# First projections on unscaled tokens: row factors applied in the evictions, bias rows copied out before the first projection's evictions

## The chip, the cores and the metric

The kernel runs on one core of a Trainium2 chip. The metric is the device time in microseconds (us) of one execution of the whole program. TensorE (PE) multiplies matrices into eight PSUM banks of 128 x 512 words. ScalarE (ACT), VectorE (DVE) and GpSimd (POOL) work beside it, and SyncE (SP) issues most transfers. Every engine goes through its own instructions in order, and engines wait for each other by semaphores.

## The reference, cut to what matters

Two transformer blocks over 512 tokens of width 1024, in 32-bit floats. The change touches the start of the first block:

```
h = rms_norm(x, norm_mix)            # x * rsqrt(mean(x*x) + eps) * gain
proj = h @ w_in
qa, ka, va, qg, kg, vg, glr, rg = split(proj)
o_a = moba_attention(qa, ka, va, rp_table)
log_a = log_sigmoid(glr @ w_gate_up + b_gate) / 16
o_g = gla_chunked(qg, kg, vg, log_a)
o_g = rms_norm(o_g, g_norm) * silu(rg)
x = x + concat(o_a, o_g) @ w_out
```

The mean is over the 1024 columns of a token, so the factor of the norm is one number for each token. A product with the weights is linear in the tokens, so that number can be multiplied in before the product or after it. Behind this come the gated linear attention, the two attentions, a cross attention and a wide MLP, and then the second block; none of that is changed.

## The kernel before

**Products.** Every 32-bit product is made of three fast ones. An operand is split into a high part (ACT copies it into `act_hi` or `w_hi`) and a low part (DVE subtracts: `act_lo`, `w_lo`), and the helper `product` issues high by high, high by low and low by high, one line each (L1211, L1212, L1213). A projection over 1024 rows takes 8 chunks k of 3 matmuls for each of 4 banks.

**Weights.** A group of 512 weight columns comes in four units, two chunks k each. The first group (units 0 to 3) is loaded at the start into `w_first`. Later units go through the two slots of `w_raw`: SP loads unit n into a slot when the count `lo_w` says that the low part of unit n - 2 is made (L1167 to L1172). ACT makes the high part (L1607), DVE the low part (L1918). So a late low part makes a late load two units on.

**Order.** `make_schedule` writes one list of steps, and `walk` has each engine go through the same list and do its part of every step. A step on which an engine has nothing to do costs it nothing, and one on which it waits holds up all that it has behind. The steps at the start are:

1. `scale` for each of four token tiles: ACT squares and sums the tile (L1720), takes logarithm and exponential (L1621, L1622), and DVE writes the scaled tile into `y` (L2024).
2. `start` 0: high and low part of weight unit 0.
3. `turn` with `of="opening"`: PE transposes the four scaled tiles (L1353), behind each tile's wait, with filler matmuls ahead of each (`warm`, L1219: 20, 5, 5, 5). ACT takes each of the 8 banks into `act_hi` (L1780), DVE into `act_lo` (L2079).
4. `start` 1: weight units 1 to 3 and the small gate weights.
5. `gemm` glaqk (the q and k of the linear attention), four banks together: chunk k is done for all four banks, then chunk k + 1. PE waits for `act_lo` of the chunk and, every second chunk, for the next unit's `lo_w`. In its first step ACT and DVE split units 4 to 7, those of the next group, vg. Each bank's eviction is behind that, on ACT for banks 0 and 2 (L1632) and on DVE for banks 1 and 3 (L1948).
6. `relbias`: PE multiplies the table of relative biases into bank 7 (L1374). DVE copies the rows out (L2103) and fills the rest (L2105). POOL first issues three loads (L2399, L2400, L2349), then writes the rows to DRAM, spreads them there into `skew_dram` (1536 KB, L2408) and later loads the skewed rows.
7. `glr`: 24 matmuls into bank 4; DVE copies them (L2084).
8. `vg`, first step: PE waits until glaqk has left bank 0 (`begin`), and for units 4 to 7 as its chunks come to them. Then the gate (PE L1369), the levels of the linear attention, and rg, qa, ka and va.

Of the kernel before, what the change touches and what calls it, by code (L numbers as in the profile page):

```python
# [27 lines left out]
F32 = mybir.dt.float32  # L28
# [3 lines left out]
ALU = mybir.AluOpType  # L32
AX = mybir.AxisListType

P = 128
# [94 lines left out]
class Step:  # L130


    def __init__(self, kind, banks, fill, *, n=0, h=0, p=None, out=None, major=None, src=None, dst=None, rows=KC,
                 half=0, first=False, splits=(), ready=None, bank=0, blk=0, mid=None,
                 after=None, tiles=TT, gains=(), chunks=(), row=None, row_n=0, qk_ready=None,
                 of=None, fused=(), units=(), tiles_free=(), held=None, roped=None, packed=None, rstd=None, xn=None, hi=None, xrows=None, smax=None, merged=None, nmax=None, part=None, sum_a=None, sq=None, nth=0, halved=False, mode=None, made=None, splits_lo=None, yg=None, banks_of=(0, TT), mean=None, sq_sum=None):
# [17 lines left out]
        self.nmax = nmax  # L154
# [3 lines left out]
class Schedule:  # L158
# [139 lines left out]
    def bank_steps(self, out, major, src, rows=KC, banks=4, halves=1, ready=None, blk=0, mid=None, dst=None, p=None,  # L298
             after=None, fused=False, pairs=False, by_tile=False, halved=None, of=None, in_parts=False, banks_at=None):
# [10 lines left out]
        for i in range(steps):  # L310
# [23 lines left out]
            else:  # L334
# [7 lines left out]
                          ready=ready if i == (1 if pairs else steps - 1 if fused else 0) else None, bank=bank, nth=b, halved=halves_ready, blk=blk, mid=mid, dst=dst, p=p,  # L342
# [100 lines left out]
def make_schedule():  # L443
# [24 lines left out]
    def transposed(tiles, gains, dst, src, of=None):  # L468

        chunks = [4, 5, 6, 7, 0, 1, 2, 3] if src == "mix" else list(range(KC))  # L470
        st = s.add("turn", range(KC), {"hi": KC}, tiles=tiles, gains=gains, dst=dst, src=src, chunks=chunks,
                   ready=all_out() if src == "mix" else None, of=of)
        return [(chunks.index(c), st.fill[chunks.index(c)], 1) for c in range(KC)]
# [362 lines left out]
def two_blocks(nc, a, out):  # L836

    s = make_schedule()
    with ExitStack() as ctx:
# [58 lines left out]
        decay = const("decay", [2, TT])  # L898

# [104 lines left out]
        bias_dram = nc.dram_tensor("bias_dram", [A_HEADS, REL], F32).ap()  # L1004
        skew_dram = nc.dram_tensor("skew_dram", [A_HEADS, P, REL], F32).ap()
# [33 lines left out]
        bias_made = sem("bias_made")  # L1039
        x_back = [sem(f"x_back{tt}") for tt in range(TT)]  # L1040
# [69 lines left out]

        def each(ap, n):

            return ap.unsqueeze(2).broadcast_to([ap.shape[0], ap.shape[1], n])
# [17 lines left out]
        def copies_of(st):  # L1131

            b, half = st.nth, st.half
            full = psum[:, st.bank, :]
            if st.out == "kx":
                return kx[:, 4 * st.blk + b, :], psum[:, st.bank, 0:M], 1.0, b % 2 == 0
            if st.out == "glaqk":
                return qk_g[:, b, :], full, G_DK ** -0.5 if b < 2 else 1.0, b % 2 == 0
            if st.out == "vg":
                return vg[:, b, :], full, 1.0, b % 2 == 0  # L1140
            if st.out == "va":
                return va[:, b, :], full, 1.0, b % 2 == 0
            if st.out == "qa":
                return qa[:, b, :], full, A_DIM ** -0.5, b % 2 == 0
            if st.out == "ka":
                return ka[:, b, :], full, 1.0, b % 2 == 0
# [61 lines left out]
        def _(pe):  # L1208
# [16 lines left out]
            def gemm(st, turn):  # L1225
# [10 lines left out]
                for k in range(st.rows):  # L1236
                    tile = k // 2 + st.half * (st.rows // 2)
                    if (st.first or st.fused) and k % 2 == 0:

                        pe.wait_ge(lo_w, at(st.units[tile][0], turn, 1))  # L1240
# [11 lines left out]
                    if k % 2 == 1 and tile in st.tiles_free:  # L1252
                        mm.then_inc(tile_done, 1)

# [57 lines left out]
            def handle(st, turn):  # L1312
# [27 lines left out]
                elif k == "turn":  # L1340
                    in_turn = lambda tt: (0, 1, 2, 4, 5, 6, 7, 3) if tt == 0 else range(KC)
                    for n, tt in [(n, tt) for tt in range(st.tiles) for n in in_turn(tt)]:
                        if st.of == "opening" and n == 0:
                            warm((20, 5, 5, 5)[tt])
# [3 lines left out]
                        if n == 0 and st.of in (None, "opening"):  # L1348
# [3 lines left out]
                        rows = y if st.of in (None, "opening") else x  # L1352
# [234 lines left out]
        def _(act):  # L1587
# [36 lines left out]
            def gemm(st, turn):  # L1624
# [5 lines left out]
                if plain is not None and plain[3]:  # L1630
                    filled()
                    act.activation(plain[0], plain[1], ACT.Copy, scale=plain[2]).then_inc(bank_free[b], 1)  # L1632
# [3 lines left out]
                elif st.out == "rg":  # L1636
                    filled()
                    act.activation(sg[:, b, :], psum[:, b, :], ACT.Sigmoid).then_inc(sig_made, 1)
# [40 lines left out]
            def handle(st, turn):  # L1679
# [31 lines left out]
                elif k == "scale_rms":  # L1711
# [9 lines left out]
                    rms(slice(tt, tt + 1), D, rstd_made)  # L1721
                elif k == "rms_x":
# [182 lines left out]
        def _(dve):  # L1905
# [32 lines left out]
            def gemm(st, turn):  # L1938
# [7 lines left out]
                if plain is not None and not plain[3]:  # L1946
                    filled()
                    dve.tensor_scalar(plain[0], plain[1], plain[2], None, ALU.mult).then_inc(bank_free[b], 1)  # L1948
# [4 lines left out]
                elif st.out == "rg":  # L1953
                    dve.wait_ge(sig_made, b + 1)
                    dve.tensor_tensor(sg[:, b, :], psum[:, b, :], sg[:, b, :], ALU.mult).then_inc(bank_free[b], 1)
# [31 lines left out]
            def handle(st, turn):  # L1987
# [93 lines left out]
                elif k == "glr":  # L2081
                    dve.wait_ge(bank_done[4], at(st.fill[0], turn, 1))
                    dve.wait_ge(bias_out, 16)
                    dve.tensor_copy(glr_t[:], psum[0:G_RANK, 4, :]).then_inc(bank_free[4], 1)  # L2084
# [16 lines left out]
                elif k == "relbias":  # L2101
                    dve.wait_ge(bank_done[7], at(st.fill[0], turn, 1))
# [237 lines left out]
        def _(pool):  # L2340
# [14 lines left out]
            def handle(st, turn):  # L2355
                k = st.kind
                if k == "tsum":
# [227 lines left out]
```

## Time and profile before

| | |
|---|---|
| median of 3 runs | 1590.48 us (1589.95 to 1591.76) |
| profiled execution, its own time | 1588.72 us |
| its span, first to last instruction | 1586.9 us |
| PE busy | 1561.5 us, 98% |
| DVE, ACT, POOL busy | 994.7, 662.9, 488.1 us |
| mean granted TensorE clock | 0.998 |

PE is busy for nearly the whole span, so what matters in a stretch is when PE can go on. Of the 25.4 us in which it isn't busy, the first 3.18 us lie ahead of its first instruction. Matmuls overlap in the trace: a 128 x 512 one is listed with 0.39 us, and the next starts 0.23 us after it.

### The profile page before, as it was taken

The numbers are of one execution on the slowest core, as the hardware profiler recorded it, in microseconds if no ns is written. First come the engines' busy times: TensorE is split into PE (matmuls) and PEld (weight loads), VectorE is DVE, ScalarE is ACT, GpSimd is POOL, SyncE is SP. The second block draws the span as 40 slices with busy tenths as digits, with TensorE's granted clock in tenths as the row PEclk, the third lists the DMA queues.
The fourth block names the chain that finished last, engine by engine and source line by source line (L and its number), as shares of the span: only waits on it lengthen the run. The fifth ranks groups of instructions, "written<-read, shape, count | busy, mean of one in ns | idle before, by whom it ended". The sixth has DMA issues, their size and how long they took to land.

```text
span 1586.9 us, 21097 instructions
## 1 busy us (share of the span) xinstructions
PE 1561.5 (98%) x7783; PEld 1308.9 (82%) x7783; DVE 994.7 (63%) x1191; ACT 662.9 (42%) x1087; POOL 488.1 (31%) x284
## 2 busy tenths in 40 slices
PE   8999989999999999999999999999999999999998
PEld 7788888888788888888888898878887988888886
DVE  5453876345477777776664747366355677777765
ACT  5352555244354443443533333634324454434432
POOL 1442000000037777762310000020014047777732
PEclk9999999999999999999999999999999999999999
DMA  6422135221312233214232122243334322213133
GB/s 242 136 80 80 41 106 179 88 80 53 133 53 107 106 107 106 106 55 153 92 106 81 54 93 83 78 162 106 98 135 137 135 107 97 88 53 123 75 109 120
DMA packets 44997, 164.34 MB, mean 104 GB/s; under 512 B 5584, under 2 KB 5800, under 8 KB 44272
## 3 DMA queue, kind: packets, MB, share of 16 engines
q1 hardware_dynamic: 40608, 144.82, 27.9%
q0 software_dynamic: 4304, 18.36, 3.3%
q8 instruction: 56, 0.92, 0.2%
q14 instruction: 29, 0.24, 0.0%
HBM read 158.88 MB, written 5.85 MB: 104 GB/s over the span
## 4 chain that ended last, share of the span: by engine, by line
PE 86%; DVE 6%; ACT 3%; issue 2%; DMA 2%; POOL 0%; DVEq 0%; SPq 0%; ACTq 0%
PE banks L1211 27%; PE banks L1213 26%; PE banks L1212 26%; DVE w_lo L1918 2%; DMA w_raw<-in_weights 2%; ACT w_hi L1607 1%; PE banks L1508 1%; PE banks L1387 1%; PE banks L1328 0%; PE banks L1570 0%; PE banks L1353 0%; PE banks L1546 0%; DVE nmax L2197 0%; PE banks L1497 0%; PE banks L1460 0%
## 5 line engine op out<-in xcount | busy, mean ns | idle before, releaser
L1211 PE MATMUL banks<-act_hi,w_hi 128*128 128x512 f32 (+1 forms) x1088 | 413.4, 380 | 2.9 <-DVE act_lo L2079 2.9
L1918 DVE TENSOR_TENSOR w_lo<-w_raw,w_hi 128x1024 fp32r<-128x1024 f32 x216 | 286.0, 1330 | 204.8 <-ACT w_hi L1607 202.5
L1213 PE MATMUL banks<-act_hi,w_lo 128*128 128x512 f32 (+1 forms) x1088 | 410.0, 377 | 0.0
L1212 PE MATMUL banks<-act_lo,w_hi 128*128 128x512 f32 (+1 forms) x1088 | 409.8, 377 | 0.0
L1607 ACT ACTIVATE w_hi<-w_raw 128x1024 fp32r<-128x1024 f32 x216 | 227.2, 1059 | 260.9 <-DMA w_raw<-in_weights 200.4
L1211 PEld LDWEIGHTS banks<-act_hi,w_hi 128*128 128x128 f32 x1088 | 204.8, 188 | 40.7 <-issue 2.3
L1213 PEld LDWEIGHTS banks<-act_hi,w_lo 128*128 128x128 f32 x1088 | 204.8, 188 | 37.9
L1212 PEld LDWEIGHTS banks<-act_lo,w_hi 128*128 128x128 f32 x1088 | 204.9, 188 | 36.5
L1211 PE MATMUL banks<-w_hi,a_hi 128*128 128x512 f32 x400 | 157.7, 394 | 2.3 <-DVE sums_y L2013 0.9
L1212 PE MATMUL banks<-w_lo,a_hi 128*128 128x512 f32 x400 | 155.9, 390 | 0.0
L1213 PE MATMUL banks<-w_hi,a_lo 128*128 128x512 f32 x400 | 155.8, 390 | 0.0
L1211 PE MATMUL banks<-w_hi,act_hi 128*128 128x512 f32 x352 | 139.8, 397 | 0.6 <-POOL act_lo L2391 0.6
L1213 PE MATMUL banks<-w_hi,act_lo 128*128 128x512 f32 x352 | 137.7, 391 | 0.0
L1212 PE MATMUL banks<-w_lo,act_hi 128*128 128x512 f32 x352 | 137.6, 391 | 0.0
L1918 DVE TENSOR_TENSOR w_lo<-t,w_hi 128x1024 fp32r<-128x1024 f32 x36 | 87.3, 2450 | 37.7 <-ACT w_hi L1607 37.7
L1211 PEld LDWEIGHTS banks<-w_hi,a_hi 128*128 128x128 f32 x400 | 75.1, 188 | 24.6 <-DVE sums_y L2013 4.0
L2365 POOL TENSOR_TENSOR t<-w_down 128x1024 f32<-128x1024 f32 x12 | 39.3, 3278 | 171.9 <-DVE act_lo L2079 171.8
L1918 DVE TENSOR_TENSOR w_lo<-w_down,w_hi 128x1024 fp32r<-128x1024 f32 x48 | 81.2, 1725 | 14.8 <-ACT w_hi L1607 14.8
L1213 PEld LDWEIGHTS banks<-w_hi,a_lo 128*128 128x128 f32 x400 | 75.1, 188 | 15.9
L1212 PEld LDWEIGHTS banks<-w_lo,a_hi 128*128 128x128 f32 x400 | 75.1, 188 | 15.0
L1211 PEld LDWEIGHTS banks<-w_hi,act_hi 128*128 128x128 f32 x352 | 73.9, 210 | 13.8 <-issue 2.0
L1213 PEld LDWEIGHTS banks<-w_hi,act_lo 128*128 128x128 f32 x352 | 73.9, 210 | 11.4
(370 smaller groups left out, 2418.4 us busy)
## 6 DMA issues: line engine op xcount, KB each, us to landing
w_raw<-in_weights SPq DMA_DIRECT2D x216, 512.0 KB, 3.6
w_down<-in_weights SPq DMA_DIRECT2D x48, 512.0 KB, 6.5
wide<-share_dram POOLq DMA_DIRECT2D x3, 1024.0 KB, 7.0
x_tok<-in_x SPq DMA_DIRECT2D x4, 512.0 KB, 5.2
w_first<-in_weights SPq DMA_DIRECT2D x4, 512.0 KB, 8.9
x_tok<-in_x POOLq DMA_DIRECT2D x4, 512.0 KB, 4.8
x_dram<-x_tok POOLq DMA_DIRECT2D x1, 2048.0 KB, 8.1
x_tok<-x_dram POOLq DMA_DIRECT2D x1, 2048.0 KB, 8.7
```

Source lines behind the costliest of these rows:

```text
L1211: pe.matmul(out_ap, lhs[0], rhs[0], start=start, stop=False)
L1212: pe.matmul(out_ap, lhs[0], rhs[1], start=False, stop=False)
L1213: return pe.matmul(out_ap, lhs[1], rhs[0], start=False, stop=stop)
L1387: mm = pe.matmul(psum[:, b, n * P // 2:(n + 1) * P // 2], lev[st.n % 2][rows, pair, tt * P:tt * P + P], right[rows, pair, tt, :, 1, :], st ...
L1508: mm = pe.matmul(psum[:, b, tt % 2 * M:tt % 2 * M + M], qx[:, 2 * st.h + e, tt * P:tt * P + P], kx[:, 2 * st.h + e, :], start=(e == 0), st ...
L1607: act.activation(w_hi[:, slot, :], landed(kind, raw), ACT.Copy).then_inc(hi_w, 1)
L1918: dve.tensor_tensor(w_lo[:, slot, :], landed(kind, raw), w_hi[:, slot, :], ALU.subtract).then_inc(lo_w, 1)
L2365: pool.tensor_tensor(t1[:], w_down[:, 1, :], w_down[:, 0, :], ALU.subtract).then_inc(sum_w, 1)
```

## The change

The steps `scale` of the tokens go. PE transposes `x` itself as soon as a tile has landed, with 10, 3, 3 and 3 fillers. A new step `rms_first`, behind `start` 1, has ACT make the row factors `rstd_x`, and POOL write them to DRAM and load them back as a row on every partition (`rstd_row`). Evictions then multiply them in: the token-major ones (vg, va, rg) by a column of `rstd_x`, the others (glaqk, qa, ka, glr) on DVE by `rstd_row`, so that banks 0 and 2 of these move from ACT to DVE. DVE's part of `relbias` becomes a step of its own, `bias_out`, in the list ahead of the glaqk steps, while the step that PE and POOL act on stays behind them. In glaqk's first chunk PE does the products of the high parts for all four banks first, once `act_hi` and `w_hi` are there, and then the two others (`first_rows`).

```diff
-    for tt in range(TT):
-        scale("x", tt, "x")
     s.add("start", n=0, splits=[s.split_of(u, []) for u in s.coming[0:1]])
-    act_ready = norm("norm_mix", "act", of="opening")
+    act_ready = transposed(TT, ["norm_mix"] * KC, "act", None, "opening")
     s.add("start", n=1, splits=[s.split_of(u, []) for u in s.coming[1:4]])
-    s.gemm("glaqk", "T", "act", ready=act_ready, fused=True)
-    s.add("relbias", (7,))
+    s.add("rms_first")
+    bias = s.add("relbias", (7,))
+    s.items.pop()
+    s.add("bias_out", of=bias)
+    s.gemm("glaqk", "T", "act", ready=act_ready, fused=True, turned=s.turned_hi)
+    s.items.append(bias)
     qk_ready = ready()
...
+            def first_rows(st, turn):
+                unit, slot = st.units[0]
+                pe.wait_ge(hi_made, at(st.turned, turn, 1))
+                pe.wait_ge(hi_w, at(unit, turn, 1))
+                for n, (x_, w) in enumerate(((act_hi, w_hi), (act_lo, w_hi), (act_hi, w_lo))):
+                    if n == 1:
+                        wait_ready(pe, st.ready[0:1], turn)
+                    if n == 2:
+                        pe.wait_ge(lo_w, at(unit, turn, 1))
+                    for one in st.fused:
...
-                            warm((20, 5, 5, 5)[tt])
+                            warm((10, 3, 3, 3)[tt])
...
+                        elif n == 0 and st.of == "opening":
+                            pe.wait_ge(x_in[tt], 16)
...
+                elif k == "rms_first":
+                    for tt in range(TT):
+                        act.wait_ge(x_in[tt], 16)
+                        then(act.activation(y[:, tt, :], x[:, tt, :], ACT.Square, accum_out=sumsq[:, tt:tt + 1]))
+                    then(act.activation(lnv[:, 0:TT], sumsq[:, 0:TT], ACT.Ln, bias=eps[:, 0:1], scale=1.0 / D))
+                    act.activation(rstd_x[:], lnv[:, 0:TT], ACT.Exp, scale=-0.5).then_inc(first_rstd, 1)
...
+                    if st.out in ("glaqk", "qa", "ka"):
+                        dve.wait_ge(spread_in, 16)
+                        dve.scalar_tensor_tensor(by_tile(plain[0]), by_tile(plain[1]), plain[2], rstd_row[:].rearrange("q (p t) -> q t p", t=TT),
+                                                 ALU.mult, ALU.mult).then_inc(bank_free[b], 1)
...
-                elif k == "relbias":
-                    dve.wait_ge(bank_done[7], at(st.fill[0], turn, 1))
+                elif k == "bias_out":
+                    dve.wait_ge(bank_done[7], at(st.of.fill[0], turn, 1))
                     dve.tensor_copy(bias_row[0:A_HEADS, 0:NEAR], psum[0:A_HEADS, 7, 0:NEAR]).then_inc(bank_free[7], 1)
...
+                if k == "rms_first":
+                    pool.wait_ge(first_rstd, 1)
+                    pool.dma_start(rstd_dram.rearrange("(q t) -> q t", t=TT), rstd_x[:]).then_inc(spread_out, 16)
+                    pool.wait_ge(spread_out, 16)
+                    pool.dma_start(rstd_row[:], rstd_dram.partition_broadcast(P)).then_inc(spread_in, 16)
```

## Rows read from the trace of the kernel before

**Rows 1.** The page, part 1: busy us, share of the span, instructions.

```profile
PE 1561.5 (98%) x7783; PEld 1308.9 (82%) x7783; DVE 994.7 (63%) x1191; ACT 662.9 (42%) x1087; POOL 488.1 (31%) x284
```

**Rows 2.** Timeline of PE, 3 to 22 us: start us, us, instructions, [idle before <-releaser].

```profile
3.18 4.53 PE L1219 MATMUL banks<-g_lo,g_hi 128*128 128x128 f32 x20 [3.18 <-DMA cols<-in_cols]
8.12 1.97 PE L1353 MATMUL banks<-ident,y_tok 128*128 128x128 f32 x8 [0.41 <-DVE y_tok L2024]
...
10.84 1.29 PE L1353 MATMUL banks<-ident,y_tok 128*128 128x128 f32 x8
...
13.88 1.06 PE L1353 MATMUL banks<-ident,y_tok 128*128 128x128 f32 x8
15.89 0.47 PE L1211 MATMUL banks<-act_hi,w_hi 128*128 128x512 f32 x1 [0.95 <-DVE act_lo L2079]
...
21.54 0.50 PE L1211 MATMUL banks<-act_hi,w_hi 128*128 128x512 f32 x1
```

**Rows 3.** SP's timeline, one row; then DMA issues at 3.5 to 3.99 us: us to landing.

```profile
3.54 2.01 SPq L1166 DMA_DIRECT2D w_first<-in_weights  x4
...
x_tok<-in_x SPq DMA_DIRECT2D x1, 512.0 KB, 7.0
w_first<-in_weights SPq DMA_DIRECT2D x1, 512.0 KB, 7.7
```

**Rows 4.** Timeline of ACT, 5 to 33 us.

```profile
5.48 1.06 ACT L1720 ACTIVATE y_tok<-x_tok 128x1024 f32<-128x1024 f32 x1 [3.47 <-DMA x_tok<-in_x]
...
11.90 1.04 ACT L1607 ACTIVATE w_hi<-w_first 128x1024 fp32r<-128x1024 f32 x1
14.28 4.74 ACT L1780 ACTIVATE act_hi<-banks,cols 128x512 fp32r<-128x512 f32 x8 [1.34 <-PE banks L1353]
18.86 3.00 ACT L1607 ACTIVATE w_hi<-w_first 128x1024 fp32r<-128x1024 f32 x3
...
32.00 1.06 ACT L1607 ACTIVATE w_hi<-w_raw 128x1024 fp32r<-128x1024 f32 x1 [8.05 <-DMA w_raw<-in_weights]
```

**Rows 5.** Timeline of DVE, 15 to 40 us.

```profile
15.00 5.36 DVE L2079 SCALAR_TENSOR_TENSOR act_lo<-banks,cols,act_hi 128x512 fp32r<-128x512 f32 x8 [0.80 <-ACT act_hi L1780]
20.27 3.48 DVE L1918 TENSOR_TENSOR w_lo<-w_first,w_hi 128x1024 fp32r<-128x1024 f32 x3
...
23.88 2.35 DVE L1918 TENSOR_TENSOR w_lo<-w_raw,w_hi 128x1024 fp32r<-128x1024 f32 x2
33.10 1.23 DVE L1918 TENSOR_TENSOR w_lo<-w_raw,w_hi 128x1024 fp32r<-128x1024 f32 x1 [6.87 <-ACT w_hi L1607]
...
38.94 0.41 DVE L2103 COPY bias_row<-banks 8x256 f32<-8x256 f32 x1
39.32 0.17 DVE L2105 MEMSET bias_row<- 8x128 f32 x1
```

**Rows 6.** Timeline of PE, 38 to 45 us: the bias product, and vg's first matmul.

```profile
38.09 0.81 PE L1374 MATMUL banks<-bucket,table 32*8 32x384 f32 x2
...
44.40 0.39 PE L1211 MATMUL banks<-w_hi,act_hi 128*128 128x512 f32 x1
```

**Rows 7.** SP's own timeline, two issues; then landings of those at 36.93 and 46.59.

```profile
25.27 0.35 SPq L1172 DMA_DIRECT2D w_raw<-in_weights  x1
...
26.41 0.34 SPq L1172 DMA_DIRECT2D w_raw<-in_weights  x1
...
w_raw<-in_weights SPq DMA_DIRECT2D x1, 512.0 KB, 3.7
...
w_raw<-in_weights SPq DMA_DIRECT2D x1, 512.0 KB, 7.1
```

**Rows 8.** Timeline of POOL, 22 to 60 us, one row.

```profile
41.94 1.12 POOL L2408 DMA_DIRECT2D skew_dram<-bias_dram  x1 [1.46 <-DMA bias_dram<-bias_row]
```

**Rows 9.** PE about 1058 us: timeline, then window 1058:1064 (the 0.72 is the granted clock).

```profile
1058.19 5.44 PE L1578 MATMUL banks<-ws_t,vt 128*128 128x128 f32 x32 [2.94 <-issue]
...
1058.00:1064.00 6.00, 5.81 (x35) 5.76 (x36) 6.00 (x3) 0.11 (x1) 5.60 (x2) 0.72 0.60 225
```

More of the change, by code:

```diff
@@ L135, in __init__ @@
                  after=None, tiles=TT, gains=(), chunks=(), row=None, row_n=0, qk_ready=None,
-                 of=None, fused=(), units=(), tiles_free=(), held=None, roped=None, packed=None, rstd=None, xn=None, hi=None, xrows=None, smax=None, merged=None, nmax=None, part=None, sum_a=None, sq=None, nth=0, halved=False, mode=None, made=None, splits_lo=None, yg=None, banks_of=(0, TT), mean=None, sq_sum=None):
+                 of=None, fused=(), units=(), tiles_free=(), held=None, roped=None, packed=None, rstd=None, xn=None, hi=None, xrows=None, smax=None, merged=None, nmax=None, part=None, sum_a=None, sq=None, nth=0, halved=False, mode=None, made=None, splits_lo=None, yg=None, banks_of=(0, TT), mean=None, sq_sum=None, turned=None):
         self.kind, self.banks, self.fill = kind, banks, fill
@@ L898, in two_blocks @@
         decay = const("decay", [2, TT])
+        rstd_x = const("rstd_x", [TT])
+        rstd_row = const("rstd_row", [T])
         cat[0] = phase
@@ L1237, in gemm @@
                     tile = k // 2 + st.half * (st.rows // 2)
+                    if k == 0 and st.turned is not None:
+                        first_rows(st, turn)
+                        continue
                     if (st.first or st.fused) and k % 2 == 0:
@@ L1253, in gemm @@
                         mm.then_inc(tile_done, 1)
+            def first_rows(st, turn):
[8 more added lines that the diff above has]
+                    for one in st.fused:
+                        if n == 0:
+                            begin(one.bank, one.fill[0], turn)
+                        lhs, rhs = w[:, slot, one.nth * P:one.nth * P + P], x_[:, 0, :]
+                        if one.major == "tok":
+                            lhs, rhs = x_[:, 0, one.nth * P:one.nth * P + P], w[:, slot, 0:512]
+                        pe.matmul(psum[:, one.bank, :], lhs, rhs, start=n == 0, stop=False)
             def contract(st, k, tile, tokens=None):
@@ L1347, in handle @@
                             begin(n, st.fill[n], turn)
-                        if n == 0 and st.of in (None, "opening"):
+                        if n == 0 and st.of is None:
                             pe.wait_ge(xn_made, at(st.src, turn, tt + 1))
+                        elif n == 0 and st.of == "opening":
+                            pe.wait_ge(x_in[tt], 16)
                         elif n == 0:
                             wait_ready(pe, st.of[tt:tt + 1], turn)
-                        rows = y if st.of in (None, "opening") else x
+                        rows = y if st.of is None else x
                         mm = pe.transpose(psum[:, n, tt * P:tt * P + P], rows[:, tt, c * P:c * P + P], ident[:])
@@ L1637, in gemm @@
                     filled()
-                    act.activation(sg[:, b, :], psum[:, b, :], ACT.Sigmoid).then_inc(sig_made, 1)
+                    act.activation(sg[:, b, :], psum[:, b, :], ACT.Sigmoid, scale=rstd_x[:, b:b + 1]).then_inc(sig_made, 1)
                     if b == TT - 1:
@@ L2083, in handle @@
                     dve.wait_ge(bias_out, 16)
[L2084 removed]
+                    dve.tensor_tensor(by_tile(glr_t[:]), by_tile(psum[0:G_RANK, 4, :]), rstd_row[0:G_RANK].rearrange("q (p t) -> q t p", t=TT),
+                                      ALU.mult).then_inc(bank_free[4], 1)
                 elif k == "gate":
```

34 lines of the change are left out of this document (23 added, 11 removed).

## The prediction, as made before the change was run

> **What bounds the kernel now.** I read the page first: PE is busy 98% of the span [rows 1], so the end moves by what PE gains or loses between its first product and the last, unless a later stall swallows it. Its longest idle times in the whole trace are the 3.18 us ahead of its first instruction and 2.94 us before 1058.19 [rows 2, 9]; neither that second one nor a shorter one is fed by a fixed time (a transfer issued at the start, say), so I take a shift made in the first 50 us as carried to the end. Then I read the timelines of the opening engine by engine.
>
> PE starts with fillers at 3.18, transposes the last scaled tile at 13.88 and starts glaqk at 15.89. It stands once more at the third chunk, at 21.54 [rows 2], when weight unit 1's low part is made: DVE makes eight `act_lo` from 15.00 and turns to that unit at 20.27 [rows 5]. From there PE runs without a gap. So the opening is set by when DVE can start `act_lo`, and the reader is to see that PE's first matmul isn't the one that counts, but the one at 21.54.
>
> The second thing to see is how far ahead the weights are. DVE makes the low parts of units 4 and 5 at 23.88, in the shade of glaqk, and SP issues the loads of units 6 and 7 at 25.27 and 26.41 [rows 5, 7]. ACT and DVE have unit 6 split from 32.00 and 33.10 [rows 4, 5], some 10 us before vg's first matmul at 44.40 [rows 6]. Here there is slack, but only because DVE gets to units 4 and 5 at 24.
>
> **The opening.** Sixteen fillers, four square-and-scale chains on ACT and four scalings on DVE go. The last token tile is issued at 3.1, just ahead of the first weights, and lands 7.0 later, at 10.1 [rows 3]. With the first tile there at 5.4, just ahead of ACT's first square at 5.48 [rows 4], PE takes two tiles at the early rate (1.97 us for 8) and two sets of three fillers (4.53 / 20 = 0.23 each): 5.5 + 2 x (1.97 + 0.68) = 10.8. The third tile goes at the later rate, 1.29, and three fillers at about half of 0.23 make 12.4 for the start of the fourth tile [rows 2]. ACT follows a tile's first transpose by 0.40 (13.88 to 14.28), so at 12.8 [rows 2, 4]. ACT is also bound by unit 0: issued at 3.54, landed 7.7 later at 11.2 [rows 3], high part 1.06 on at 12.3 [rows 4], low part on DVE 1.23 more [rows 5], 13.6. So DVE starts `act_lo` at 13.6 in place of 15.00: a gain of 1.4. The products of the high parts start PE at about 13.5, more than 2 us earlier than 15.89, but PE then stands longer ahead of the third chunk, since DVE's eight `act_lo` (5.36) and unit 1's low part come no sooner than 1.4 earlier. High parts first is therefore worth nothing beyond the 1.4. Bounds: 0.5, if all four tiles went at the early rate (fourth tile at 5.5 + 3 x 2.65 = 13.5, `act_lo` at 14.5), and 1.8 if unit 0 lands a little sooner than its row says. I take 1.4, since both chains come to it.
>
> **The row factors.** ACT's `rms_first` is four squares (1.06 each and about 0.3 for sum and signal), a logarithm and an exponential: some 6 us behind `start` 1, which ends at about 20.5, so about 26 [rows 4]. That pushes the high parts of units 4 and 5 to 28, still before anyone asks. POOL's two small transfers take, by the landings of 3.7 to 7.1 for far larger ones [rows 7], until 40 at the very most; DVE asks for `rstd_row` after 44. So these are hidden, and if that cover went, the price is what is late past 44. POOL's three later loads slip by 5 us, and none is asked for before 49. The evictions that multiply cost 0.67 (5.36 / 8, the same instruction from PSUM) [rows 5]; the strided read of the row is not in the trace, I bound it by 0.67 and twice that, and take 0.67, since the instruction is the same: only the first one stands on PE's path, the others are done in the 5.4 us of a step. DVE's extra evictions of qa and ka, four of 0.67, have idle time of DVE to go into, as it is busy 63% of the span [rows 1]. Nothing for both; without that cover they would cost 2.7.
>
> **The bias rows.** This is the part that costs. DVE's copy waits for bank 7, which PE fills only behind the whole of glaqk. Before, DVE stood in that wait with nothing else due. Now `bias_out` stands ahead of glaqk's first step, and that step holds the low parts of units 4 to 7 and, behind them, all four evictions of glaqk. So units 4 and 5, made at 23.88 before, wait until PE's bias product is done, and units 6 and 7 aren't even loaded. Behind DVE wait SP (`lo_w`), ACT (unit 6's landing) and PE (bank 0 for vg).
>
> The chain, with the opening's 1.4 taken off: DVE's copy starts at 38.94 - 1.4 = 37.54 and the two bias instructions take 0.55 (to 39.49) [rows 5]. From the low part of unit 4 to the issue of unit 7's load it is 26.41 - 23.88 = 2.53 [rows 5, 7]. Then the landing, L. Then ACT, 1.10 to DVE's start (32.00 to 33.10), DVE 1.23 [rows 4, 5], and 0.89 from the start of the first eviction to PE's matmul, as `act_lo` at 15.00 let PE go at 15.89 [rows 2, 5]. Without L that is 37.54 + 6.30 = 43.8. PE, done with glr, would be at vg at 44.40 - 1.4 = 43.0 [rows 6]. So PE stands L + 0.8.
>
> L: a load with nothing beside it took 3.7, one issued while the bias rows were being spread in DRAM took 7.1 [rows 7]. The spreading was issued 3.0 after DVE's copy started (41.94 against 38.94) [rows 5, 8]; unit 7's load comes 3.1 after it (0.55 + 2.53). They start together. I take the middle, 5.4, as the load finds the spreading only beginning. So PE starts vg at 49.2 instead of 44.40: +4.8, with +3.1 and +6.5 as the bounds.
>
> The Trainium skill (DMA: Bandwidth & Descriptors, section on the anatomy of one DMA) fits a transfer as about 2.0 us and its bytes at 436 GB/s, 3.2 us for such a load, an estimate; the trace's best is 3.7. By it alone the stall would be 2.2 us shorter than I take it. The row with 7.1 speaks against using it here.
>
> **The clock behind the stall.** PE then stands 6.2 us. The only idle time of this kind in the trace is 2.94 us before 1058.19, and in the six microseconds behind it the mean granted clock was 0.72: it fell to 1.2 GHz and came back to 2.4, at a price of 6.00 x 0.28 = 1.7 us [rows 9]. A stall twice as long should do that too. Bounds: nothing, and 3.5, half of the 7 us from 3.18 to about 10 in which the opening's matmuls ran at the early rate [rows 2]. I take 1.7.
>
> **Sum.** -1.4 + 6.2 + 1.7 = +6.5 us. On the profiled execution, 1588.72, that gives 1595.2. This lies 1.8 below the median of the runs, 1590.48, so the median becomes 1597.0. About 0.2%, 3.2 us, is what a measurement of this kernel can tell from no change.
>
> **Rivals.**
> *Stall without the clock's fall* (0.20). For it: the rest of the trace keeps 2.4 GHz. Against it: rows 9. +4.8, 1595.3, with 1593.6 to 1597.
> *The stall doesn't come, or is short* (0.12). It needs DVE to get past `bias_out` before PE has done the bias product, or the loads to be nearly free. The change then keeps its 1.4 and gives 1589.1, which counts as no change. What decides it is L: with the clock's fall the loss passes 3.2 us from L = 2.1, without it from L = 3.8. Against it: the best L here is 3.7, and before, DVE's copy started only when the product was done (38.09 + 0.81, copy at 38.94) [rows 5, 6].
> *The thinner fillers leave the array slow* (0.05). Then glaqk's first 24 matmuls run at half rate and add up to 5 us more: 1602. Against it: up to 10 us PE is as busy as before, since transposes fill the place of fillers. The Trainium skill (TensorE: Matmul & The Clock Gate, Part 1) says that sustained activity releases the throttle; the opening's rows agree.
> *No stall, and an opening that gives over 3.2* (0.03). Unit 0 lands at 11.2 [rows 3], and from there ACT, DVE and the eight `act_lo` leave at most 1.8; no row supports more. It would give 1587.
>
> My forecast has 0.60. Slower by over 0.2%: 0.60 + 0.18 + 0.05 = 0.83. Within: 0.02 of the first rival and the second's 0.12, 0.14. Faster: 0.03. The range runs from 1592.2, short of the low bound without the clock's fall, to 1601.0, which is +6.5 for the stall with L = 7.1, 3.5 for the clock, and a little over; below it lie the second and the last rival, above it the third.
>
> **What would show it.** Right: DVE's COPY of `bias_row` at about 37.5 with the low parts of units 4 to 7 behind it, SP's loads of units 6 and 7 at 39.5 and 40.6, PE idle from about 43 to 49 ahead of vg, a granted clock under 1 behind that, third chunk of glaqk at 20.2. It would be wrong if DVE's low parts still ran at 24, if PE found bank 0 free, or if a later stall shrank by several microseconds.

## The result, and the profile after

The changed kernel takes 1600.07 us, median of 5 runs (1598.71 to 1601.49), against 1590.22 (1589.82 to 1591.76) for the kernel before in 5 runs: 9.85 us slower, ratio 1.0061 with a 95% interval of 1.005 to 1.0072. The forecast of 1597.0 is 3.1 short. The median lies inside its range, 0.9 below the upper end; two of the five runs lie above it. The profiled execution took 1601.49 with a span of 1599.7. It is the slowest of its five, and that of the kernel before was among its fastest, so the spans differ by 12.8.

PE's timeline of the changed kernel, 11 to 62 us, answers to [rows 2, 6]; L1285 is `first_rows`, L1222 the first line of `product`, L1408 the bias product, L1403 the gate:

```profile
11.38 1.06 PE L1387 MATMUL banks<-ident,x_tok 128*128 128x128 f32 x8
14.95 1.07 PE L1285 MATMUL banks<-act_hi,w_hi 128*128 128x512 f32 x2 [2.52 <-DVE act_lo L2129]
16.17 0.50 PE L1285 MATMUL banks<-act_hi,w_hi 128*128 128x512 f32 x1 [0.15 <-DVE act_lo L2129]
16.83 0.79 PE L1285 MATMUL banks<-act_hi,w_hi 128*128 128x512 f32 x1 [0.16 <-DVE act_lo L2129]
17.42 1.91 PE L1285 MATMUL banks<-act_lo,w_hi 128*128 128x512 f32 x4
19.13 1.56 PE L1285 MATMUL banks<-act_hi,w_lo 128*128 128x512 f32 x4
20.53 0.40 PE L1222 MATMUL banks<-act_hi,w_hi 128*128 128x512 f32 x1
...
23.28 0.39 PE L1222 MATMUL banks<-act_hi,w_hi 128*128 128x512 f32 x1
...
39.70 0.81 PE L1408 MATMUL banks<-bucket,table 32*8 32x384 f32 x2
...
52.59 0.79 PE L1222 MATMUL banks<-w_hi,act_hi 128*128 128x512 f32 x1 [6.42 <-DVE qk_g L1992]
...
60.63 1.98 PE L1403 MATMUL banks<-glr_t,w_gu 16*128 16x512 f32 x4
```

Three things are to be seen. The fourth tile is transposed from 11.38, a microsecond earlier than forecast (12.4), and then PE stands 2.52 us: even the products of the high parts wait for `act_lo`. The bias product is at 39.70, against 38.09 in [rows 6]: the opening costs 1.6 us in place of giving 1.4. And ahead of vg PE stands 6.42 us (forecast 6.2), so vg starts 8.2 us later than in [rows 6]. DVE's timeline, 14 to 57 us, answers to [rows 5]:

```profile
14.05 5.36 DVE L2129 SCALAR_TENSOR_TENSOR act_lo<-banks,cols,act_hi 128x512 fp32r<-128x512 f32 x8
19.33 3.48 DVE L1960 TENSOR_TENSOR w_lo<-w_first,w_hi 128x1024 fp32r<-128x1024 f32 x3
...
40.54 0.41 DVE L2154 COPY bias_row<-banks 8x256 f32<-8x256 f32 x1 [17.53 <-PE banks L1408]
41.02 2.28 DVE L1960 TENSOR_TENSOR w_lo<-w_raw,w_hi 128x1024 fp32r<-128x1024 f32 x2
...
50.35 1.23 DVE L1960 TENSOR_TENSOR w_lo<-w_raw,w_hi 128x1024 fp32r<-128x1024 f32 x1 [2.10 <-ACT w_hi L1641]
51.49 3.99 DVE L1992 SCALAR_TENSOR_TENSOR qk_g<-banks,rstd_row 128x512 f32<-128x512 f32 x4
55.40 1.10 DVE L2134 TENSOR_TENSOR glr_t<-banks,rstd_row 16x512 f32<-16x512 f32 x1
```

DVE stands 17.53 us in the wait of the bias rows. Units 4 and 5, split at 23.88 in [rows 5], come at 41.02 behind it. An eviction takes 1.0 us (3.99 / 4). The last link is SP's load of unit 7, the answer to [rows 7]. It was issued at 43.48, and the DMA issues of that moment (median us from issue to landing at the end) show 5.8:

```profile
w_raw<-in_weights SPq DMA_DIRECT2D x1, 512.0 KB, 5.8
```

The row factors themselves are hidden, as forecast, on POOL's timeline; the spreading of the bias rows comes at 43.53, with unit 7's load ([rows 8] before):

```profile
25.91 0.58 POOL L2410 DMA_DIRECT2D rstd_dram<-rstd_x  x1 [19.32 <-ACT rstd_x L1763]
27.92 0.54 POOL L2412 DMA_DIRECT2D rstd_row<-rstd_dram  x1 [1.43 <-DMA rstd_dram<-rstd_x]
...
43.53 1.12 POOL L2464 DMA_DIRECT2D skew_dram<-bias_dram  x1 [1.46 <-DMA bias_dram<-bias_row]
```

The windows of PE (stretch, its length, PE busy and matmuls, granted clock, then DMA share and GB/s) show the clock fall to its lower level, 1.2 GHz, twice, once in the opening and once while PE stands:

```profile
16.00:17.00 1.00, 0.69 (x3) 0.87 0.94 377
17.00:18.00 1.00, 1.00 (x3) 0.50 0.07 25
18.00:19.00 1.00, 1.00 (x4) 0.50 0.00 0
19.00:20.00 1.00, 1.00 (x4) 0.50 0.00 0
20.00:21.00 1.00, 1.00 (x6) 0.92 0.00 0
...
51.00:52.00 1.00, 0.00 (x0) 0.50 0.87 356
...
57.00:58.00 1.00, 1.00 (x4) 0.65 0.11 44
```

From vg's first matmul to the gate it is 8.04 us (52.59 to 60.63), and 5.53 in the kernel before (44.40 to its gate at 49.93): the second fall costs 2.5. At the gate the changed kernel is 10.7 us behind. That goes with the 9.85 of the medians. The rest of the 12.8 came later in this one execution: some 0.9 in short waits between 500 and 900 us, 0.9 in the wait of [rows 9] (3.84 in place of 2.94), and 0.6 behind that. At 213 us PE stands as it does before the change (2.12 us, to 202.93). Here the clock fell behind it, to a mean of 0.83 in 210 to 220, and in the kernel before it stayed at 1.00; but PE then waits 0.89 us for DVE (to 206.96) and does not in the changed kernel, and by 238 us the distance is 10.5, no more than at the gate. PE's row in the changed kernel:

```profile
213.62 0.39 PE L1222 MATMUL banks<-mem_hi,w_hi 128*128 128x256 f32 x1 [2.07 <-ACT kx L1668]
```

### The profile page after: what moved, and what is told of

It reads as the page before. It is cut to its first block, busy times and chain, and to the rows that moved or that the text cites. A ratio compares the mean times of both kernels' runs of the same rounds, so it can differ in the third digit from the quotient of the medians.

```text
span 1599.7 us, 21080 instructions
## 1 busy us (share of the span) xinstructions
PE 1565.7 (98%) x7767; PEld 1310.6 (82%) x7767; DVE 1001.7 (63%) x1193; ACT 659.0 (41%) x1075; POOL 488.6 (31%) x286
## 4 chain that ended last, share of the span: by engine, by line
PE 85%; DVE 6%; DMA 3%; ACT 3%; issue 2%; SPq 0%; POOL 0%; DVEq 0%; ACTq 0%
PE banks L1222 26%; PE banks L1223 26%; PE banks L1224 26%; DMA w_raw<-in_weights 2%; DVE w_lo L1960 2%; ACT w_hi L1641 1%; PE banks L1542 1%; PE banks L1421 1%; DMA w_first<-in_weights 1%; PE banks L1360 0%; PE banks L1604 0%; PE banks L1580 0%; DVE nmax L2248 0%; PE banks L1531 0%; PE banks L1494 0%
## 5 line engine op out<-in xcount | busy, mean ns | idle before, releaser
L1222 PE MATMUL banks<-act_hi,w_hi 128*128 128x512 f32 (+1 forms) x1084 | 411.7, 380 | 1.9 <-DVE act_lo L2129 1.9
L1222 PEld LDWEIGHTS banks<-act_hi,w_hi 128*128 128x128 f32 x1084 | 204.1, 188 | 39.3 <-DVE act_lo L2129 1.2
L1222 PE MATMUL banks<-w_hi,a_hi 128*128 128x512 f32 x400 | 158.1, 395 | 3.0 <-DVE sums_y L2063 1.2
L1222 PE MATMUL banks<-w_hi,act_hi 128*128 128x512 f32 x352 | 140.9, 400 | 7.0 <-DVE qk_g L1992 6.4
L1222 PEld LDWEIGHTS banks<-w_hi,a_hi 128*128 128x128 f32 x400 | 75.0, 188 | 26.1 <-DVE sums_y L2063 4.5
L1222 PEld LDWEIGHTS banks<-w_hi,act_hi 128*128 128x128 f32 x352 | 74.5, 212 | 20.8 <-DVE qk_g L1992 6.8
```

Of the source, the lines that this page charges most:

```text
L1222: pe.matmul(out_ap, lhs[0], rhs[0], start=start, stop=False)
```

## The experiments

**E1, the bias rows back behind glaqk.** Everything else as changed.

```diff
-    s.add("bias_out", of=bias)
     s.gemm("glaqk", ..., turned=s.turned_hi)
     s.items.append(bias)
+    s.add("bias_out", of=bias)
```

> The changed kernel with one part undone: DVE copies the bias rows out behind glaqk's evictions again. Theory: the low parts of weight units 4 to 7 held behind the bias wait cost it all of the stall ahead of vg (6.4 us of idle PE at 46.17 to 52.59) and the slow clock behind it (2.5 us). Expected: no idle time of PE ahead of vg, loads of units 6 and 7 issued before 32, the opening as in the changed kernel (bias product at 39.7), time 1600.1 - 8.9 = 1591, about as before. Rival: DVE's four evictions with the row factors, or the row's way through DRAM, hold bank 0 as well; then PE still stands 3 us or more ahead of vg and the time is 1594 or above.

Measured: 1590.81 (11 runs, 1590.03 to 1593.73), ratio 1.0006 (0.9997 to 1.0015). There is no stall ahead of vg, and DVE is back at units 4 and 5 at 26.91. The opening stays slow, with the bias product at 40.08 and the clock down behind 17. DVE's timeline, and then windows of PE:

```profile
26.91 2.36 DVE L1960 TENSOR_TENSOR w_lo<-w_raw,w_hi 128x1024 fp32r<-128x1024 f32 x2 [3.57 <-ACT w_hi L1641]
```

```profile
16.00:18.00 2.00, 1.69 (x5) 0.90 0.57 227
18.00:20.00 2.00, 2.00 (x7) 0.50 0.00 0
```

So the place of the bias rows is 9.3 of the 9.85 us.

**E2, the order of the first chunk back.** Bias rows early, as changed; the products of the first chunk bank by bank.

```diff
-    s.gemm("glaqk", ..., fused=True, turned=s.turned_hi)
+    s.gemm("glaqk", ..., fused=True)
```

> The changed kernel with one part undone: in glaqk's first chunk PE does three products for a bank and then the next bank, as before. Theory: banks 0 to 3 come free one by one as DVE makes act_lo, so the high products of four banks wait for four act_lo, and the other eight matmuls come behind that; the chunk takes longer and PE is so thin in it that the clock falls. Expected: no fall of the clock in 12 to 22 us, glaqk's third chunk at 20.5 in place of 23.3, the stall ahead of vg unchanged, time 1600.1 - 2.8 = 1597.3. Rival: the 16 fillers that went let the clock fall, whatever the order; then the granted clock is still under 0.9 between 16 and 20 us and the gain is 1.3 us or less.

Measured: 1597.85 (5 runs, 1597.52 to 1598.76), ratio 1.0047 (1.0033 to 1.0061). PE starts at 14.97, no earlier and no later than in the changed kernel, but is 2.5 us ahead of it at the bias product, and the granted clock is 1.00 throughout 12 to 22. Rows of PE's timeline:

```profile
20.62 0.50 PE L1222 MATMUL banks<-act_hi,w_hi 128*128 128x512 f32 x1
...
37.17 0.81 PE L1408 MATMUL banks<-bucket,table 32*8 32x384 f32 x2
...
50.49 0.79 PE L1222 MATMUL banks<-w_hi,act_hi 128*128 128x512 f32 x1 [6.85 <-DVE qk_g L1992]
```

The third chunk at 20.62 is the one forecast at 20.2. High parts first is a loss: 2.2 us by the medians. vg starts 2.1 us earlier and not 2.5, because the stall is 0.4 longer: unit 7's load took 6.2 us here and 5.8 in the changed kernel.

**E3, the fillers back** (20, 5, 5, 5), everything else as changed.

```diff
-                            warm((10, 3, 3, 3)[tt])
+                            warm((20, 5, 5, 5)[tt])
```

> The changed kernel with 20, 5, 5 and 5 fillers in place of 10, 3, 3 and 3. Theory: the clock falls in glaqk's first chunk because PE gets only one matmul for each act_lo there, not because fillers went; more fillers only end the transposes later. Expected: fourth tile's transposes at about 13.9, first matmul at 15.5 or later, granted clock still under 0.9 in some two microseconds between 16 and 21 us, time 1600 or above (1599 to 1602). Rival: with the fillers back the clock holds 2.4 GHz in the opening and the time is 1598.5 or below.

Measured: 1599.67 (4 runs, 1598.25 to 1600.49), ratio 1.0062 (1.0047 to 1.0078). The idle time ahead of the first product is only 1.02, and the clock falls all the same (windows of PE):

```profile
16.00:18.00 2.00, 1.69 (x5) 0.83 0.57 225
18.00:20.00 2.00, 2.00 (x7) 0.50 0.03 8
```

The fillers aren't what costs the opening its clock. The stall ahead of vg is 5.08 us here, shorter by as much as unit 7's load is quicker (4.4 us).

**E4, the early bias rows alone,** put into the kernel before.

```diff
-    s.gemm("glaqk", "T", "act", ready=act_ready, fused=True)
-    s.add("relbias", (7,))
+    bias = s.add("relbias", (7,))
+    s.items.pop()
+    s.add("bias_out", of=bias)
+    s.gemm("glaqk", "T", "act", ready=act_ready, fused=True)
+    s.items.append(bias)
...
-                elif k == "relbias":            # DVE's part
+                elif k == "bias_out":
```

> The kernel before with one part of the change alone: DVE's copy of the bias rows stands ahead of glaqk's steps. Theory: this alone makes the stall. Chain from the copy at 38.9: units 4 and 5, the load of unit 7 issued at 42.0, landed by 47.5, low part at 49.9, first eviction at 50.6: PE idle from 44.4 to about 50.8, and a slow clock behind it; time 1590.2 + 6.4 + 2.5 = 1599. Rival: the stall needs the row factors as well (their wait, and four evictions on DVE in place of two), and ACT's evictions of banks 0 and 2 take part of it; then the time is below 1595.

Measured: 1596.22 (5 runs, 1595.37 to 1597.4), ratio 1.0038 (1.0024 to 1.0052). Slower, as expected, but by 5.9 and not 9. PE's row shows a stall about half as long, and ended by ACT:

```profile
48.70 0.50 PE L1214 MATMUL banks<-w_hi,act_hi 128*128 128x512 f32 x1 [3.53 <-ACT qk_g L1635]
```

Unit 7 was issued at 42.48 and landed 4.6 later, at 47.1. From there ACT makes the high part (1.06) and evicts bank 0 at once, so PE goes on 1.6 us after the landing. In the changed kernel, where all four evictions are DVE's, bank 0 waits for the high part, the low part and a longer eviction: 3.3 us (49.3 to 52.59). The row factors by themselves cost nothing that is clear of the noise (E5 and E6 below), but on this path they make the stall 1.7 us longer. 1.2 more is the landing, which differs as much among executions of the same chain (4.4 in E3, 6.2 in E2).

**E5, both back** (the edits of E1 and E2; unscaled tokens, row factors and fewer fillers stay).

```diff
-    s.add("bias_out", of=bias)
-    s.gemm("glaqk", ..., turned=s.turned_hi)
+    s.gemm("glaqk", ...)
     s.items.append(bias)
+    s.add("bias_out", of=bias)
```

> The changed kernel without the early bias rows and without the high parts first; the unscaled tokens, the row factors and the fewer fillers stay. Theory: this keeps the gain of an earlier first eviction: glaqk's third chunk at about 20.5 in place of 21.5 before, no stall ahead of vg, time 1590.2 - 1.0 = 1589.2. Rival: the fewer fillers let the clock fall in the opening also so; then the granted clock is under 0.9 between 16 and 20 us and the time is 1590.5 or above.

Measured: 1590.05 (11 runs, 1588.52 to 1591.15), ratio 0.9998 (0.9989 to 1.0007). The bias product is at 36.87 and the gate at 48.71, each 1.2 us earlier than before the change; the medians keep 0.25 of it. DVE now writes the bias rows behind the evictions, and `glr_t` is held up by their transfer (DVE's timeline):

```profile
43.29 0.41 DVE L2154 COPY bias_row<-banks 8x256 f32<-8x256 f32 x1
...
46.08 1.04 DVE L2134 TENSOR_TENSOR glr_t<-banks,rstd_row 16x512 f32<-16x512 f32 x1 [2.25 <-DMA bias_dram<-bias_row]
```

**E6, unscaled tokens and row factors alone** (E5 with E3's fillers).

```diff
-                            warm((10, 3, 3, 3)[tt])     # on E5
+                            warm((20, 5, 5, 5)[tt])
```

> The changed kernel with fillers (20, 5, 5, 5), order of the first chunk and the place of the bias rows as before: what stays is the unscaled tokens with the row factors in the evictions. Theory: the gain of the earlier opening comes from both fewer fillers and unscaled tokens; with 35 fillers ACT reaches the transposed banks about 1.0 us later than with 19, so the gain over the kernel before is nearly nothing: 1590.3, within 1 us. Rival: the row factors by themselves cost something later (four evictions of 1.0 us on DVE in place of 0.6 to 0.7, and four more for qa and ka); then it is 1591.5 or above.

Measured: 1590.88 (11 runs, 1590.4 to 1592.68), ratio 1.0007 (0.9998 to 1.0016). DVE's timeline in this profile shows what the bias rows do when they come late:

```profile
48.94 1.05 DVE L2134 TENSOR_TENSOR glr_t<-banks,rstd_row 16x512 f32<-16x512 f32 x1 [4.03 <-DMA bias_dram<-bias_row]
```

PE waits 0.58 for it at the gate, which starts at 50.04, with a granted clock of 0.74 in the 4 us behind. That takes back the opening's gain in this execution, in which the bias rows' transfer took longer than in E5 (DVE waits 4.03 us for it, and 2.25 there). That it is worth something to have them out ahead of the evictions isn't shown: with that, E9 (below) is 0.8 slower than E1, and E10 0.8 faster than E5. Ahead of the splits of the weights is what costs.

**E7, the stall filled.** The changed kernel, with 55 filler matmuls on PE behind glr, which nothing reads.

```diff
                     mm.then_inc(bank_done[4], 1)
+                    busy(55)    # 55 times: pe.matmul(psum[:, 6, T - P:T], g_hi[:, 0, :], g_lo[:, 0, :], start=True, stop=True)
```

> The changed kernel with 55 filler matmuls of 128 columns behind glr, ahead of vg, into a bank that isn't in use; nothing else. Theory: PE stands some 6.4 us there, the clock falls to 1.2 GHz in it and vg's first step takes 2.5 us longer. With about 5.9 us of fillers in the gap the clock stays at 2.4 GHz: vg starts where it did (52.6), its first step takes 5.5 in place of 8.0, time 1600.1 - 2.5 = 1597.6. Rival: the slow stretch belongs to something else (PE's loads of weights behind late low parts, or DMA traffic); then the first step still takes 7 us or more and the time stays at 1600.

Measured: 1598.07 (4 runs, 1597.34 to 1599.98), ratio 1.0053 (1.0037 to 1.0068), 2.0 us faster than the changed kernel. vg starts when it did, and the clock is whole. PE's timeline, and then its window at 50 to 54:

```profile
52.73 0.50 PE L1222 MATMUL banks<-w_hi,act_hi 128*128 128x512 f32 x1 [0.61 <-DVE qk_g L1998]
```

```profile
50.00:54.00 4.00, 3.39 (x25) 1.00 0.94 272
```

The gate is at 58.41, 2.2 us earlier than in the changed kernel. With four and five runs the times of the two kernels overlap, so it is this row rather than the medians that shows the clock's fall to be a cost of its own, some 2 us beside the stall.

**E8, the spreading later.** The changed kernel, where POOL holds the spreading in DRAM until unit 7 is split.

```diff
+                    pool.wait_ge(lo_w, 8)
                     pool.dma_start(skew_dram, each_row)
```

> The changed kernel with POOL starting to spread the bias rows in DRAM only when the low parts of units 4 to 7 are made. Theory: unit 7's load takes 5.8 us to land because it runs beside the spreading; without it it lands 3.7 after its issue, PE stands 2.1 us shorter ahead of vg (4.3), time 1600.1 - 2.1 = 1598. Rival: unit 7 is held up by unit 6's load just ahead of it; then it still takes 5 us or more and the time stays at 1600.

Measured: 1598.93 (4 runs, 1597.92 to 1600.4), ratio 1.0058 (1.0043 to 1.0074): 1.1 us less than the changed kernel, where 2.1 was expected, and the runs of the two overlap. Unit 7, issued at 43.17, landed after 4.2; PE's timeline:

```profile
50.75 0.75 PE L1222 MATMUL banks<-w_hi,act_hi 128*128 128x512 f32 x1 [4.89 <-DVE qk_g L1992]
```

The stall is 1.5 us shorter and the landing 1.6, so the stall follows the landing, but the clock falls behind 4.89 us as it does behind 6.42 (0.60 in 50 to 54). That the spreading is what lengthens the landing is not shown by this one execution: beside the spreading the same load took 5.8 (changed kernel), 6.2 (E2), 4.4 (E3), 4.6 (E4) and 6.0 (E7), and 4.2 is only just below these. The rival, unit 6's load 1.1 us ahead, is still there at 4.2, so it costs little.

**E9, the bias rows behind the splits and ahead of the evictions,** for what E5 and E6 showed.

```diff
-    s.add("bias_out", of=bias)
...
                     split(st, turn)
+                if st.out == "glaqk" and st.nth == 0:
+                    bias_rows(s.bias, turn)    # wait for bank 7, copy, memset, as bias_out
```

> The changed kernel with DVE's copy of the bias rows one place further back: behind the low parts of units 4 to 7, still ahead of glaqk's evictions; all else kept. Theory: only the low parts behind the bias wait made the stall, not the evictions behind it. Expected: no idle time of PE ahead of vg, the opening as in the changed kernel (clock under 0.9 for some microseconds between 16 and 22 us), time as with the bias rows put back, 1590.8 (1590 to 1592). Rival: the evictions behind the bias wait hold bank 0 as well; then PE stands 1 us or more ahead of vg and the time is 1592.5 or above.

Measured: 1591.63 (11 runs, 1589.08 to 1593.0), ratio 1.0007 (0.9998 to 1.0016). DVE's timeline shows the wait of 17.53 us down to 0.30, and `glr_t` waits for PE alone:

```profile
39.62 0.41 DVE L1983 COPY bias_row<-banks 8x256 f32<-8x256 f32 x1 [0.30 <-PE banks L1408]
...
40.10 3.84 DVE L2000 SCALAR_TENSOR_TENSOR qk_g<-banks,rstd_row 128x512 f32<-128x512 f32 x4
45.28 1.04 DVE L2142 TENSOR_TENSOR glr_t<-banks,rstd_row 16x512 f32<-16x512 f32 x1 [1.34 <-PE banks L1224]
```

**E10, E9 with the old order of the first chunk.**

```diff
-    s.gemm("glaqk", ..., fused=True, turned=s.turned_hi)     # on E9
+    s.gemm("glaqk", ..., fused=True)
```

> As the kernel with the bias rows behind the low parts, and with three products for a bank and then the next bank in glaqk's first chunk. Theory: as with both parts undone, since the bias rows only have to leave the low parts alone: 1590.0, third chunk at about 20.4, gate at about 48.7. DVE's copy of glr no longer waits for the bias rows' transfer and runs some 2 us earlier than there, off PE's path. Rival: the earlier spreading of the bias rows runs beside the loads of the next units and costs something: 1591 or above.

Measured: 1589.24 (11 runs, 1587.85 to 1591.03) against 1590.49 (33 runs), ratio 0.9993 (0.9984 to 1.0002). It is the best version, 2.4 us faster than E9 and 10.8 than the changed kernel, and not clearly apart from the kernel before. PE's timeline has the bias product and the gate 1.2 us earlier than before the change:

```profile
36.89 0.81 PE L1408 MATMUL banks<-bucket,table 32*8 32x384 f32 x2
...
48.73 1.98 PE L1403 MATMUL banks<-glr_t,w_gu 16*128 16x512 f32 x4
```

**E11, the row of factors in the order of the tokens,** on E10: the evictions read it contiguously, and the 2 KB transfer to DRAM goes in single words.

```diff
-  pool.dma_start(rstd_dram.rearrange("(q t) -> q t", t=TT), rstd_x[:])
+  pool.dma_start(rstd_dram.rearrange("(t q) -> q t", t=TT), rstd_x[:], allow_slow_non_contiguous=True)
-  dve.scalar_tensor_tensor(by_tile(plain[0]), by_tile(plain[1]), plain[2], rstd_row[:].rearrange("q (p t) -> q t p", t=TT),
+  dve.scalar_tensor_tensor(plain[0], plain[1], plain[2], rstd_row[:],
```

> As the one with the chunk order put back, and the row of factors lies in token order on every partition, so that DVE's evictions read it without a stride of 16 bytes (its small transfer to DRAM is then made of single words). Theory: the stride is why glaqk's evictions took 1.0 us each (3.97 for four) and not 0.67; in order they take 0.7 or less. They are off PE's path here, so the time stays at 1590. Rival: the price of 1.0 comes from three operands with one in PSUM, not from the stride; then they still take 1.0. Second rival: the transfer in single words is late; then DVE's evictions start later than 39.5 and PE may stand ahead of vg.

Measured: 1592.73 (11 runs, 1591.43 to 1593.84), ratio 1.0015 (1.0005 to 1.0024), 3.5 us slower than E10: the stride is the price of the evictions, as the theory has it, and the second rival came true as well. An eviction takes 0.60 us in place of 0.96, but the transfer of 2 KB takes 10.1 in place of 1.7, and the weights loaded beside it land late: ACT gets unit 6 at 39.31, and PE stands 0.90 us ahead of vg. DVE's timeline, ACT's, and the DMA issues:

```profile
43.52 2.41 DVE L2000 SCALAR_TENSOR_TENSOR qk_g<-banks,rstd_row 128x512 f32<-128x512 f32 x4
```

```profile
39.31 1.06 ACT L1641 ACTIVATE w_hi<-w_raw 128x1024 fp32r<-128x1024 f32 x1 [12.15 <-DMA w_raw<-in_weights]
```

```profile
rstd_dram<-rstd_x POOLq DMA_DIRECT2D x1, 2.0 KB, 10.1
```

**E12, E11 with 9 fillers ahead of the fourth tile** in place of 3, to see whether the opening's clock can be made safe.

```diff
-                            warm((10, 3, 3, 3)[tt])     # on E11
+                            warm((10, 3, 3, 9)[tt])
```

> As the one with the row in token order, and with 9 fillers in place of 3 ahead of the fourth tile. Theory: the run times of the kernels with the thin opening lie about 1 us above what their profiles gain, because PE stands 2.0 us ahead of glaqk and the clock falls there in some executions. The fourth tile's transposes come 0.7 us later, just when ACT is ready for them (12.5), and PE stands 1.4 us. Expected: mean granted clock 0.998 as before in most executions, time 1589.1, 1.1 below the kernel before. Rival: the fall doesn't hang on this gap; then clock and time are as without the six fillers, 1590.

Measured: 1591.78 (11 runs, 1590.86 to 1593.62), ratio 1.001 (1.0001 to 1.0019), 1.0 us less than E11. In the profiled execution PE stood 2.11 us before its first product, and the clock fell although the first chunk was dense (windows of PE):

```profile
16.00:18.00 2.00, 2.00 (x7) 0.50 0.47 188
18.00:20.00 2.00, 2.00 (x8) 0.69 0.00 0
```

So these fillers don't keep the clock up in every execution, and the time expected, 1589.1, is missed by 2.7. Whether they help is open: the mean granted clocks of E12's eleven runs (0.997 or 0.998) lie a little above those of E11's (0.994 to 0.998).

## Why the prediction was right, and where it was wrong

**The bias rows: right, link by link.** From DVE's copy to vg's first matmul the forecast had 6.30 + L = 11.7 us, and it is 12.05 (40.54 to 52.59). The copy starts 0.84 behind the bias product (0.85 in [rows 5, 6]), the load of unit 7 is issued 2.94 behind the copy (forecast 3.08), L is 5.8 (taken 5.4), and ACT, DVE and PE follow in 1.09, 1.14 and 1.10. E1 takes the cause away and with it 9.3 us; with the old chunk order the same move is worth 7.8 (E2 to E5), and from the changed kernel to E9 8.4. What this step lacked is in E4: the evictions moved from ACT to DVE stand in the same chain, and are 1.7 us of the stall. The sum had the first of them in its chain, with 0.89 from its start to PE's matmul (1.10 measured); it priced the chain of the changed kernel rightly, but called the move itself free.

**L: right in size, its reason not shown.** It was 5.8 for 5.4, and in all five profiles with the same chain beside the spreading it was 4.4 to 6.2, between the ends that the forecast gave (3.7 and 7.1). With the spreading held back it was 4.2 (E8). This points the way that the forecast had it, but one execution so close to the others can't carry it, and a spread of 1.8 us among them makes the hit within 0.4 partly luck.

**The clock behind the stall: right, a little small.** 2.5 us at the gate in place of 1.7, inside the bounds, and 2.0 by E7. It had fallen while PE stood, ahead of vg's first matmul.

**The opening: wrong, and this is the error of the forecast.** The step that failed is "The products of the high parts start PE at about 13.5 ... High parts first is therefore worth nothing beyond the 1.4." The forecast saw what each product reads and not where it writes. Banks 0 to 3 hold the transposed tokens, and glaqk writes into the same banks. So the high by high product of bank b must wait until DVE has taken `act_lo` b out of it, however early `act_hi` and `w_hi` are. The releaser says so in each row of L1285. DVE frees a bank every 0.67 us. In the old order PE has three matmuls, 3 x 0.23 = 0.69 us, for each bank freed, and just keeps pace. In the new order it has one of 0.23, and the eight others queue behind the fourth. The first chunk takes 5.6 us (14.95 to 20.53) in place of some 2.7. Against E2, where the third chunk starts at 20.62, it starts at 23.28, 2.7 later. The clock windows add up to 1.7 of that (0.13 + 0.50 + 0.50 + 0.50 + 0.08); the 1.0 left is the order by itself. By the medians the order costs 2.2 (changed kernel to E2), 0.8 (E1 to E5) and 2.4 (E9 to E10). In all six profiles with high parts first the clock fell in the opening, with 1.02 to 3.06 us of idle time ahead; of the eight with the old order it fell in one, E12. That thin work behind an idle time brings the fall is what these profiles bear out, one execution of each; E12 shows that it isn't the only way.

The remaining part of the opening was right in mechanism: with the old order DVE starts `act_lo` at 14.08 (E2) in place of 15.00, and the third chunk comes 0.9 (E2) to 1.3 us (E11) earlier. The 1.4 was too much by what unit 0 landed late, at 11.75 for the forecast 11.2; in E11 it is there at 11.39. Of the two chains of which the forecast said that both come to 1.4, only that of unit 0 holds: the fourth tile's transposes began at 11.38, not 12.4.

**The terms side by side.** Opening +1.6 for -1.4; chain and idle time 6.42 for 6.2; clock 2.5 for 1.7; at the gate +10.7 for +6.5. Of the 4.2 missing, 3.0 are the opening. By the medians +9.85. That the time still lies in the range is luck in part: the opening's bounds (a gain of 0.5 to 1.8) don't hold its loss of 1.6, and what covered it was room that the range had for L and for the clock.

**The evictions** took 1.0 us and not 0.67, inside the bound of twice that. The strided read is the reason: E11 reads the same numbers in order and takes 0.60. The row of factors is read at every fourth word, 16 bytes apart. The Trainium skill (SBUF — State Buffer, section on the DMA port swizzle) says that SBUF has lines of 16 bytes, that accesses to one line run at full bandwidth and that each access which crosses to a new one pays; the trace agrees, at 0.96 against 0.60 us for 512 elements.

**The rivals.** The stall without the clock's fall is out by the windows; E7 is that case made by hand, at 1598.07 (with the slow opening, for which that rival had no term). The thin fillers aren't the cause of the slow opening (E3); its effect, PE at half rate in the first chunk, was what that rival described, from another cause. The stall did come, and the opening gave nothing.

**What the forecast called carried to the end** was nearly so. The wait of [rows 9], which the profile puts down to issue, is not fixed: it is 2.8 to 3.1 in the kernel before and in E3, E4, E6, E7 and E12, and 3.6 to 4.2 in the changed kernel, E1, E2, E5 and E8 to E11. The second set is just those with the 19 fillers of the change and no other instruction added to PE. About 1 us of a gain made in the opening goes there. That it hangs on the number of instructions is read off these 14 profiles and wasn't tried by itself; it stays open.

## What to carry to other kernels

A step that only waits must not stand ahead of work that others live on: ask for each step on an in-order engine what is queued behind it, down to the loads that its count releases two units on. Before products are reordered, ask where each one writes as well as what it reads: a bank that still holds its own input frees at the pace of the engine that empties it, and here the order that does all the work of a bank as it comes free is the one that hides that pace. When work is moved to another engine because that engine is idle, look at whether it then lies behind something that can stall.

## What the runs showed of the hardware

- A contiguous operand of VectorE against one at a stride of 16 bytes: 0.60 and 0.96 to 1.0 us for 128 x 512 from PSUM.
- 2 KB written in single words took 10.1 us, against 1.7 in pieces of 16 bytes, and the weight loads issued by SP meanwhile landed late: ACT stood 12.15 us for one (11.85 in E12, which has the same transfer). The Trainium skill (DMA: Bandwidth & Descriptors, Specifications) names 512 bytes as the least for full rate; both pieces are below it, and the trace shows a sixfold difference between them.
- TensorE's clock fell behind 2.1 to 3.1 us without work in some executions and not in others with about the same idle time (2.11 us in E12, 2.27 in E11), and also behind 1.0 us followed by single matmuls 0.67 us apart (E3). The stand of 2.0 to 2.1 us for ACT's `kx`, at 202 to 214 us, is in all 14 profiles: the clock fell behind it in ten, and not in the kernel before, E9, E10 and E12. In the changed kernel that fall cost nothing on balance, since a wait for DVE came close behind.
- The clock column of the windows can miss the slow start: it lists 1.00 from 3 us on in the kernel before, while eight transposes take 1.97 us at 8.12 and 1.06 at 13.88. There the rates tell it.
